# One fused instruction for mask and maximum, a 128-row meta product, and a rounded split sample bias in a decoder's attention stage

## What is computed

```python
s = q . k * scale + cum[query] - cum[key]     # cum: running sum of the log forget values
p = softmax(where(mask, s, -1e30))            # mask: key position <= query position
o = p . v
```

## Time and profile before

| | us |
|---|---|
| median of three runs (lowest, highest) | 1995.82 (1989.45, 1998.66) |
| time of the profiled execution | 1992.6 |
| its span, first to last instruction | 1990.7 |
| PE busy in it | 1915.0 (96%) |
| DVE busy | 1032.3 (52%) |
| ACT busy | 691.4 (35%) |
| POOL busy | 440.4 (22%) |

### The profile page before, as it was taken

The page is one execution under the profiler, slowest core; times in us unless marked ns, Lnnn a source line. Parts: engine busy times, 40 slices in busy tenths (PEclk is TensorE's granted clock), DMA queues, the critical chain, the costliest instruction groups (busy, mean ns, idle before and its releaser), DMA issues.

```text
span 1990.7 us, 35893 instructions
## 1 busy us (share of the span) xinstructions
PE 1915.0 (96%) x14783; PEld 1770.3 (89%) x14783; DVE 1032.3 (52%) x1170; ACT 691.4 (35%) x898; POOL 440.4 (22%) x106
## 2 busy tenths in 40 slices
PE   7999999999999999999999999889998999999998
PEld 6979969979889999999999989855555999999998
DVE  4445245245446865454542534567674566646452
ACT  5232232232224335251431442244554342515251
POOL 2302412312303411212132333100001332121212
PEclk9999999999999999999999999989998999999999
DMA  5341441442245646464632222478785222223231
GB/s 164 128 164 49 139 151 62 139 137 70 101 169 155 184 139 203 139 202 139 202 94 85 66 64 64 175 275 281 294 297 203 86 85 85 85 85 100 68 106 47
DMA packets 206574, 272.76 MB, mean 137 GB/s; under 512 B 17442, under 2 KB 169378, under 8 KB 206242
## 3 DMA queue, kind: packets, MB, share of 16 engines
q1 hardware_dynamic: 184866, 216.83, 34.1%
q10 hardware_dynamic: 21488, 53.46, 7.3%
q0 software_dynamic: 80, 0.52, 0.1%
HBM read 244.33 MB, written 59.68 MB: 153 GB/s over the span
## 4 chain that ended last, share of the span: by engine, by line
PE 68%; issue 16%; DVE 6%; POOL 4%; ACT 2%; DMA 2%; ACTq 1%; SPq 0%; DVEq 0%; POOLq 0%
PE PS L816 12%; PE PS L817 12%; PE PS L818 12%; POOL w_lo L756 4%; PE PS L832 4%; PE PS L834 4%; PE PS L833 4%; PE PS L895 3%; PE PS L896 3%; PE PS L897 3%; PE PS L1378 2%; PE PS L1333 1%; DVE k_page_t L2406 1%; PE PS L1313 1%; PE PS L1319 1%
## 5 line engine op out<-in xcount | busy, mean ns | idle before, releaser
L756 POOL TENSOR_TENSOR w_lo<-w_raw,w_hi 128x2048 fp32r<-128x2048 f32 (+2 forms) x101 | 439.2, 4348 | 1519.3 <-ACT w_hi L1483 1519.3
L1483 ACT ACTIVATE w_hi<-w_raw 128x2048 fp32r<-128x2048 f32 (+2 forms) x101 | 178.1, 1764 | 640.5 <-PE PS L818 411.4
L816 PE MATMUL PS<-hidden_hi,w_hi 128*128 128x296 f32 (+1 forms) x1024 | 304.8, 298 | 0.7 <-DVE hidden_tmp L2175 0.6
L818 PE MATMUL PS<-hidden_hi,w_lo 128*128 128x296 f32 (+1 forms) x1024 | 305.1, 298 | 0.0
L817 PE MATMUL PS<-hidden_lo,w_hi 128*128 128x296 f32 (+1 forms) x1024 | 304.7, 298 | 0.0
L816 PE MATMUL PS<-x_hi,w_hi 128*128 128x296 f32 (+1 forms) x896 | 269.8, 301 | 5.3 <-DVE x_lo L1934 2.7
L817 PE MATMUL PS<-x_lo,w_hi 128*128 128x296 f32 (+1 forms) x896 | 268.9, 300 | 0.0
L818 PE MATMUL PS<-x_hi,w_lo 128*128 128x296 f32 (+1 forms) x896 | 268.2, 299 | 0.0
L895 PE MATMUL PS<-w_hi,x_hi 128*128 128x256 f32 x800 | 226.2, 283 | 0.4 <-DVE fox_gate L2327 0.4
L897 PE MATMUL PS<-w_lo,x_hi 128*128 128x256 f32 x800 | 225.2, 281 | 0.0
L896 PE MATMUL PS<-w_hi,x_lo 128*128 128x256 f32 x800 | 225.0, 281 | 0.0
(11 more groups left out here) (306 smaller groups left out, 3870.4 us busy)
## 6 DMA issues: line engine op xcount, KB each, us to landing
w_raw<-in_w_mlp_up SPq DMA_DIRECT2D x32, 1024.0 KB, 5.4
staged_k<-in_cache_k SPq DMA_DIRECT2D x256, 128.0 KB, 3.0
w_raw<-in_w_mlp_down SPq DMA_DIRECT2D x32, 1024.0 KB, 5.1
k_page<-staged_k SPq DMA_DIRECT2D x64, 512.0 KB, 5.8
v_page<-in_cache_v ACTq DMA_DIRECT2D x56, 512.0 KB, 6.4
w_raw<-in_w_ret_in SPq DMA_DIRECT2D x24, 1024.0 KB, 5.5
sample_state<-in_state_ret SPq DMA_DIRECT2D x32, 512.0 KB, 5.4
out_state_ret_sample<-sample_state ACTq DMA_DIRECT2D x32, 512.0 KB, 4.4
```

The costliest lines, as they stand in the source:

```text
L756: pool.tensor_tensor(lo, raw, hi.bitcast(F32), ALU.subtract).then_inc(lo_done, 1)
L816: pe.matmul(o, wh[:, w], xh[:, t, cols], start=(t == 0), stop=False)
L818: last = pe.matmul(o, wl[:, w], xh[:, t, cols], start=False, stop=(t == kt - 1))
L1483: act.activation(part(WH[n.slot], n, kt), part(WR[n.slot], n, kt), ACT.Copy).then_inc(hi_done, 1)
```

## The change

- **Fused mask and maximum.** `maximum` becomes one `tensor_tensor_reduce` over all `n` columns: it adds a wide mask `ZM` (zeros with the causal block at columns 400 to 527, so that a shifted slice of it fits either parity and any `n`), multiplies by -1, writes the result back to PSUM and gives the minimum. `exp` reads the negated scores with `scale=-1.0`. The semaphore `masked` goes. `ZM` is filled by a memset and a copy ahead of the loop.
- **128-row meta product.** `VM` and `PTM` get 128 rows; rows 32 to 127 of `PTM` are zeroed once ahead of the loop. The 32 live rows are copied as before.
- **Sample bias from rounded parts.** The running sums are split into a rounded high and a low part, stacked on 128 partitions: `CLA` for sequences 0 to 3, `CLB` for 4 to 7; the selection matrix is rounded too (`SELR`). `bias_part` is then one product, 128 rows deep. The parts are made by ACT copies and DVE subtractions: `SELR` and the high part of `CLA` among the last weight splits of ACT; its low part on DVE behind the third V projection; `CLT`, `CLB` just ahead of the loop, where ACT waits for `cum_lo1` and DVE for `cum_hi1`, which itself comes after `k_stored`.
- **Seven value buffers.** `NVS` goes from 8 to 7. SP no longer loads an eighth page; `v_next` runs for every page below 64, so ACT issues 57 loads in place of 56, each one page later in the order than before: page 7 of a sequence is now loaded in its own slot 2, after page 0 of that sequence has been used.
- Buffers move: `new_k_rows`, `logf`, `o_tok`; the selection matrix is loaded by a DMA of its own.

The diff, without the moves of buffers and the semaphores' names:

```diff
-NKS, NVS = 4, 8
+NKS, NVS = 4, 7
...
-                if b == 0:
-                    sp.wait_ge(qb_done, 1)
-                    v_page(6)
-                    sp.wait_ge(kn_done, 1)
-                    v_page(7)
+                if b == 0:
+                    sp.wait_ge(qb_done, 1)
+                    v_page(6)
...
             def bias_part(b, bank, a, e):
-                r = slice(64 * (b // 4), 64 * (b // 4) + 64)
-                pe.matmul(PS[:, bank, 0:e - a], cf("selb")[r, P * (b % 4):P * (b % 4) + P], CL[r, a:e], start=True,
+                cum = CLA if b < 4 else CLB
+                pe.matmul(PS[:, bank, 0:e - a], SELR[:, P * (b % 4):P * (b % 4) + P], cum[:, a:e], start=True,
                           stop=False, skip_group_check=True)
             def bias(b):
                 if b > 0:
                     pe.wait_ge(sex_done, b)
+                else:
+                    pe.wait_ge(cum_lo0, 1)
+                if b == 4:
+                    pe.wait_ge(cum_done1, 1)
...
+            act.activation(SELR[:], SELF[:], ACT.Copy)
             act.activation(NSR[:], cf("negsel"), ACT.Copy).then_inc(rounded, 1)
...
             w_hi(Blk(N_V + 3))
+            act.wait_ge(cum_scanned, 1)
+            act.activation(CLA[0:64, :], CL[0:64, :], ACT.Copy).then_inc(cum_hi0, 1)
...
-                act.activation(own_probs(par, n), score_cols(par, n), ACT.Exp, bias=NM[:, par:par + 1],
+                act.activation(own_probs(par, n), score_cols(par, n), ACT.Exp, scale=-1.0, bias=NM[:, par:par + 1],
...
-                    if 0 <= b < DB - 1:
+                    if 0 <= b and vn < NPAGE * DB:
...
             act.wait_ge(k_stored, 48)
             act.wait_ge(table_in, 16)
+            act.activation(CLT[64:P, :], CL[64:P, :], ACT.Copy).then_inc(cum_hi1, 1)
+            act.wait_ge(cum_hi1, 1)
+            act.wait_ge(cum_lo1, 1)
+            act.activation(CLB[64:P, :], CLT[64:P, :].bitcast(F32), ACT.Copy).then_inc(cum_done1, 1)
...
             evac_tok(Blk(N_V + 2), VV, 2)
+            dve.wait_ge(cum_hi0, 1)
+            dve.tensor_tensor(CLA[64:P, :], CL[0:64, :], CLA[0:64, :].bitcast(F32), ALU.subtract).then_inc(cum_lo0, 1)
...
-                own = score_cols(par, n)[:, m - P:m] if par == 0 else score_cols(par, n)[:, n - P:n]
-                dve.tensor_tensor(own, own, cf("causal"), ALU.add).then_inc(masked, 1)
-                dve.wait_ge(masked, 2 * j + par + 1)
-                dve.tensor_reduce(NM[:, par:par + 1], score_cols(par, n), AX, ALU.max, negate=True).then_inc(mx_done, 1)
+                at = NKEY + (NMETA if par == 0 else 0) - n
+                x = score_cols(par, n)
+                dve.tensor_tensor_reduce(out=x, in0=x, in1=ZM[:, at:at + n], op0=ALU.add, op1=ALU.min, scale=-1.0,
+                                         scalar=-NEG, accum_out=NM[:, par:par + 1]).then_inc(mx_done, 1)
...
             evac_tok(Blk(N_V + 3), VV, 3)
+            dve.memset(ZM[:], 0.0).then_inc(zeros_set, 1)
+            dve.memset(PTM[:], 0.0).then_inc(zeros_set, 1)
+            dve.wait_ge(zeros_set, 2)
+            do(dve.tensor_copy(ZM[:, NKEY - P:NKEY], cf("causal")))
             dve.transpose(KN[:], KNS[:].rearrange("p (i j c) -> p j i c", i=2, j=8)).then_inc(kn_done, 1)
             dve.wait_ge(k_stored, 48)
             dve.wait_ge(tok_turned, 2 * KT)
+            dve.wait_ge(cum_hi1, 1)
+            dve.wait_ge(cum_lo0, 1)
+            dve.tensor_tensor(CLB[0:64, :], CL[64:P, :], CLT[64:P, :].bitcast(F32), ALU.subtract).then_inc(cum_lo1, 1)
```

More of the change, by code:

```diff
@@ L70 @@
 FOX, FOX_N = columns([("causal", P), ("newmask", DB * NSAMP), ("own", NSAMP), ("headpick", 4),
-                      ("selb", 4 * P), ("negsel", FH), ("rep", P)])
+                      ("negsel", FH), ("rep", P)])
+SEL_N = 4 * P
 def constants():
@@ L147, in constants @@
     put(fox, FOX, "rep", (np.arange(P)[None, :] % FH == np.arange(FH)[:, None]) * 1.0)
-    return {"c_keep": keep, "c_ret": ret, "c_fox": fox}
+    return {"c_keep": keep, "c_ret": ret, "c_fox": fox, "c_sel": sb.reshape(P, SEL_N).astype(f)}
 class Blk:
@@ L317, in program @@
         TK, at = place("fox_k_tok", [P, 5, D], TK0)
-        LF, at = place("logf", [FH, T], at)
+        KNS, at = place("new_k_rows", [P, 512], at)
+        LF, _ = place("logf", [FH, T], R1 + 8 * T)
         CU, at = place("cum_parts", [P, NKEY], at, F32R)
+        CLA, _ = place("sample_cum_parts0", [P, SK], R1 + 8 * T, F32R)
+        CLB, _ = place("sample_cum_parts1", [P, SK], at, F32R)
         CL, at = place("sample_cum", [P, SK], at)
         CF, at = place("c_fox_sb", [P, FOX_N], at)
+        SELF, _ = place("select_b", [P, SEL_N], at)
+        SELR, at = place("select_b_r", [P, SEL_N], at, F32R)
         NSR, at = place("negsel_r", [P, FH], at, F32R)
@@ L326, in program @@
         RM, at = place("row_inv", [P, 4], at)
+        OS, _ = place("o_tok", [P, DH], at)
         LS, at = place("sample_logf", [P, NSAMP], at)
@@ L337, in program @@
         PP, at = place("probs", [P, 2 * NKEY], at)
-        PTM, at = place("probs_t_meta", [2 * NMETA, P], at)
+        PTM, at = place("probs_t_meta", [P, P], at)
+        CLT, _ = place("sample_cum_hi1", [P, SK], at, F32R)
         PB, at = place("sample_probs", [P, SK], at)
@@ L341, in program @@
         OX, at = place("o_by_head", [P, 4, DH], at)
-        OS, at = place("o_tok", [P, DH], at)
         KN, at = place("new_k_t", [P, 8, NSAMP], at)
+        ZM, at = place("mask_wide", [P, NKEY + NMETA], at)
         assert at <= R0 + 4 * KT * T
-        VM, _ = place("meta_v_by_head", [2 * NMETA, KT, P], R1)
-        KNS, _ = place("new_k_rows", [P, 512], R1 + 8 * T)
+        VM, _ = place("meta_v_by_head", [P, KT, P], R1)
         KP, at = place("k_page_t", [P, NTURN, 8, P], TK0)
@@ L471, in program @@
         rounded = sem("rounded")
+        cum_scanned = sem("cum_scanned")
+        cum_hi0 = sem("cum_hi0")
+        cum_lo0 = sem("cum_lo0")
+        cum_hi1 = sem("cum_hi1")
+        cum_lo1 = sem("cum_lo1")
+        cum_done1 = sem("cum_done1")
         s_ready = sem("s_ready")
-        masked = sem("masked")
+        zeros_set = sem("zeros_set")
         mx_done = sem("mx_done")
@@ L680, in _ @@
             sp.dma_start(CF[:], io["c_fox"]).then_inc(fox_in, 16)
+            sp.dma_start(SELF[:], io["c_sel"]).then_inc(fox_in, 16)
             with nc.allow_non_contiguous_dma(reason="the gain of the keys, on every partition"):
@@ L691, in _ @@
                 weights(Blk(N_K + j), w_kvf[:, :, BW * j:BW * j + BW])
-            sp.wait_ge(fox_in, 16 * 3)
+            sp.wait_ge(fox_in, 16 * 4)
             def k_page(kn):
@@ L779, in _ @@
             mlp(N_MLP0, 0)
-            pool.wait_ge(fox_in, 16 * 3)
+            pool.wait_ge(fox_in, 16 * 4)
             pool.indirect_dma_start(LFP[:], None, io["cache_logf"].rearrange("n k h -> n (k h)"),
@@ L1197, in new_logf @@
                         .then_inc(small_ready, 1)
-            pe.wait_ge(fox_in, 16 * 3)
+            pe.wait_ge(fox_in, 16 * 4)
             unit_tok(Blk(N_Q), tile=fox_sums)
@@ L1840, in probs_copy @@
                 act.wait_ge(pt_ready, 3 * j + 3)
-                act.activation(PTM[:], PS[0:2 * NMETA, 7, 2 * P:3 * P], ACT.Copy).then_inc(pt_evac, 1)
+                act.activation(PTM[0:2 * NMETA, :], PS[0:2 * NMETA, 7, 2 * P:3 * P], ACT.Copy).then_inc(pt_evac, 1)
             def exp_s(b):
@@ L2359, in _ @@
             dve.wait_ge(small_done, 1)
-            do(dve.tensor_tensor_scan(CL[:, PAST:SK], ones.to_broadcast([P, NSAMP]), LS[:], CL[:, PAST - 1:PAST],
-                                      ALU.mult, ALU.add))
+            dve.tensor_tensor_scan(CL[:, PAST:SK], ones.to_broadcast([P, NSAMP]), LS[:], CL[:, PAST - 1:PAST],
+                                   ALU.mult, ALU.add).then_inc(cum_scanned, 1)
             evac_tok(Blk(N_K + 2), TK, 2)
```

5 lines of the change are left out of this document (2 added, 3 removed).

## The result

The changed kernel takes 1984.6 us, the median of 15 runs (1977.31 to 1988.72), where the kernel before takes 1998.66 beside it (15 runs, 1989.45 to 2006.43). The ratio is 0.9934, with a 95% interval of 0.9918 to 0.9951. On another chip the ratio was 0.9956 (0.9935 to 0.9977). The forecast was 1984.8, a gain of 11.0 us.

The account below looks back on a forecast made before the run. DVE bounds slot 0, PE the rest, with ACT close behind in slot 1. Terms 3.2 + 0.4 + 0.25 + 6.2 + 0.46 + 1.0 - 0.5 = 11.0 us, from 1995.8 to 1984.8 (1979 to 1990; with rivals 1977 to 1998).

Parts of the forecast that it names:

- slot 0, turns 2 to 8: From end of `scores` to L1300, held by DVE: fused maxima save 3.2 us; turn 8's shorter bias adds 0.25.
- turn 1, slot 0: Turn 1 begins at the lower clock, so PE's shorter 64-column bias counts there: 0.4 us gained.
- slot 1, turns 1 to 7: L1300 to slot 2's first `probs_t`: PE's bias saves 1.45, ACT becomes the bound at 0.88 a turn; 6.2 us.
- slot 1, turn 8: No bias left, PE waits for ACT's chain, so the two fused maxima count in full: 0.46 us.
- meta product: Slots 2 and 3: 128-row depth gains 0 to 0.16 us a pair; half taken, 1.0 us in seven turns.
- end of turn 8: Last turn: page 7's load goes out behind `v_used` of page 0 and ACT's last copies, lower clock; 0.5 us lost.
- x: Extra cost of the fused maximum for writing out its minimum on DVE: between 0 and 0.19 us, 0.10 taken.
- The first rival: Fused instruction takes two cycles a column, so the bias gains nothing: 1996.6 us, no change; chance 0.12.
- the room: Slot 1: `probs_copied` lets PE go on 0.44 us before PE comes there, so PE's saving counts for that much.
- The third rival: Slot 1: ACT's chain does not shorten, exponentials wait for something else, only 0.44 gained a turn; 1988 to 1992; chance 0.20.
- The second rival: Page 7 lands late at `page_values(b, 7)` in eight turns; landing of 9.3 loses 20.8 us: 2010.6; chance 0.10.
- the cover of loads: Loop start: DVE's later waits, 5.4 us together, cover a first page turn at 1287.0; cost 0, without cover 3.4.

Follow-up runs that it names:

- the two half kernels: Changed kernel with mask and maximum as two instructions again: 1995.18 us, ratio 0.9992; changed kernel with the fp32 bias again: 1990.83 us, ratio 0.9965.
- last page ahead of stores: Changed kernel with page 7 of sequences 0 to 6 issued by SP, page 63 on ACT ahead of stores and `w_hi`: 1982.25 us, ratio 0.9921.
- seven buffers once more: Kernel before with seven value buffers and nothing else changed, executed and profiled a second time: 1999.43 us, ratio 1.0000.
- the second run of the changed kernel: The changed kernel, unaltered, run and profiled again on another chip: 1989.07 us, ratio 0.9956 to the kernel before.

## Why the prediction was right, and where it was not

The mechanism stood, and each rival's condition could be read off. The terms, from the two traces (rounded one by one, the sum from the exact values):

| term, us gained | forecast | traces |
|---|---|---|
| slot 0, turns 2 to 8 | 3.2 + 0.25 | 6 x 0.60 + 0.54 = 4.1 |
| turn 1, slot 0 | 0.4 | 0.37 |
| slot 1, turns 1 to 7 | 6.2 | 7 x 0.75 = 5.3 |
| slot 1, turn 8 | 0.46 | 0.56 |
| meta product | 1.0 | 0.1 (slots 2 and 3 where no page is late) |
| late pages, turns 1 to 4 | 0 | -1.9 |
| start | 0 | -0.6 |
| end of turn 8 | -0.5 | -1.2 |
| after the projection begins | 0 | 0.2 |
| sum | 11.0 | 6.8 |

**The fused maximum** was sized too dear: x is 0.03 on average (0.50 and 0.54 beside the reduction's 0.49), not 0.10. The bound from ACT's accumulator held, but the better end was zero. The Trainium skill, VectorE: DVE Perf Modes, Two Vector instructions with no wait between them, says that there are two instructions; the trace agrees, and shows that the second, 141 ns long, lies beside the next. The first rival falls with 1.05 ns a column. The half throughput that the prediction cites beside this rival is not seen here, with one source in PSUM; no run shows whether this instruction, `CUSTOM_DVE_ANT_0` in the trace, is of the family meant there.

**Slot 1** did change hands, as PE's 0.57 for ACT and the two half kernels show. It gained 0.75 and not 0.88. ACT's chain became shorter by 0.56 rather than 0.46, so the term that was mis-sized is the room: in the timeline PE starts `probs_t` 0.71 behind the start of ACT's last copy before the change, and 0.52 behind it where it truly waits. The room was 0.19. I had built the hand-over from the copy's length and a step of 0.08 that no row showed, 0.34 in all, and it takes 0.52. The bias itself saves 1.34 (1.91 to 0.57, where 0.46 was forecast), which is still more than the stretch gained. The third rival falls. PE's `probs_t` in the timeline of the kernel before, without a wait:

```profile
1377.06 1.09 PE L1296 MATMUL PS<-c_keep_sb,probs 128*128 128x128 f32 x8
```

**The meta product** failed as a term. L1319 at either depth takes 0.42 a pair, and L1393 in front of it 0.97 as before: nothing moved. Half of an unknown gain was the wrong choice where the row that it was compared with, L1060, stands among products of its own kind. The Trainium skill, TensorEngine Tiling (Array Packing), Tiling Modes, says that a change of mode drains the engine; by that rule the term is 0, and the trace agrees with it.

**Seven buffers** were not free, and the step that failed is the landing. When PE would want the page was right to 0.3 (6.7 forecast; 1384.96 - 1378.00 = 7.0 measured); 6.3 us of landing, 6.0 to 6.4 in all such turns of the kernel before, became 5.5 to 7.4, with 6.9 and over in the turns that lose time. The run with page 7 on SP points to what the landing hangs on, a key page in the air; such a page was in the air in the kernel before as well, and why the landing now scatters is open. The second rival thus came true in part, at a tenth of its price.

**The start** cost 0.6, of which 0.1 is the execution's own. The first page turn came at 1287.25 (1287.0 forecast), and the cover of loads held as argued.

**The end** held 1.2 against 0.5. The cause was not the one named: no page is late there. In the kernel before GpSimd's subtraction already held `o_tok`, so the 1.1 us that slots 0 and 1 of turn 8 gained could not reach the end of the tail unless the subtraction came sooner too. It did not: with the load of page 63 ahead of it on ACT, `w_hi` starts 5.84 behind the start of ACT's last copy of a sample's probabilities in place of 4.58, and the subtraction 20.70 into the turn in place of 20.54. So the forecast's 0.25 and 0.46 for turn 8 were not to be had, and I had not followed ACT's queue to that engine.

**The missing six.** The traces give 6.8 of gain, the ratio 13. A gap of that sign stands in twelve of the thirteen traces that can be set against the one trace of the kernel before, from 0.9 us (last page ahead of stores) to 11.8 (seven buffers once more); only before with seven buffers and page 7 by SP has one of 2.9 the other way, and its traced execution was itself 5.8 under its median. So most of the gap belongs to the one execution of the kernel before that was traced. The granted clock that the record has for each execution says in what it was quick: its mean clock was 0.990, where 31 executions of that kernel on the chip of the second run of the changed kernel average 0.987, and those with a lower clock take longer (a median of 1994 us at 0.989 and over, of 1999 at 0.986 and 0.987). The changed kernel's fifteen executions average 0.990. So the ratio holds some microseconds of clock for which the forecast had no term; where in the program the other executions spend them, and whether the change has a part in it, no trace shows, as the kernel before was traced once.

That the forecast, 1984.8, lies 0.2 from the median is therefore in part luck: by the traces its 11.0 was 4 us too high, and the base that it was taken from, 1995.8, lay 2.9 below the median of the fifteen runs. Its ends, gains of 17 and 6, do not follow from its terms either, which give some 15 and 7.

## What to carry to other kernels

Where two engines end a stretch within half a microsecond of each other, cost both edits together: here each alone gave 0.2 and 0.6 us a turn, and both 1.4. Measure the room between them from a hand-over in which one truly waits, not from the length of the instruction that is waited for. A buffer taken away is a load issued later, and its landing depends on what else is in the air; look at the order of all queues around it, in the last turn too, where stores join in.

## What the runs showed of the hardware

- DVE's fused add, minimum and accumulation over PSUM and SBUF costs 1.05 ns a column, no more than a reduction alone, and its accumulator read of 141 ns lies wholly beside the next instruction.
- A 512 KB page landed in 3.7 us on one queue and in 7.4 on another at the same place of a turn. A key page issued 0.4 us behind it or 2.3 ahead of it is the difference that the issues show; on that second queue, with no key page in the air, it took 3.6 us.
- A DVE operation on 128x64 took 2.16 us beside GpSimd's subtraction and 0.25 without it. In nine of nine traces in which the two met it ended 0.05 us behind the subtraction, after 0.95 to 3.37 us, while the reduction just ahead of it took its 0.57 beside the same subtraction.
- The granted clock fell from 1.00 to under 0.6 for some 10 to 11 us in the middle of the loop, with PE busy and a plain turn ahead of it, in three of three traces of the kernel before with seven buffers. The cause is open.
